# In the attention phase, a projection or a half-chunk stands ahead of the score step in each turn, instead of behind it

## The reference

```python
def fox_prompt(q, k, v, logf):
    c = jnp.cumsum(logf, axis=1).transpose(0, 2, 1)
    ...
    def block(i):
        ...
        s = jnp.einsum('bqhd,bkhd->bhqk', qb, k).astype(jnp.float32) * scale
        s = s + (cb[..., :, None] - c[..., None, :])
        s = jnp.where(qpos[:, None] >= kpos[None, :], s, -jnp.inf)
        p = jax.nn.softmax(s, axis=-1).astype(v.dtype)
        return jnp.einsum('bhqk,bkhd->bqhd', p, v)
...
    m = jax.nn.sigmoid(g_a) * (a @ w_pa) + jax.nn.sigmoid(g_b) * (b @ w_pb)
```

## Time and profile before

| | |
|---|---|
| median of three runs | 1940.32 us |
| profiled execution, its own time | 1940.35 us |
| its span | 1938.6 us |
| TensorE busy | 1886.9 us (97%) |
| VectorE, ScalarE, GpSimd busy | 962.6, 679.1, 521.3 us |
| mean granted TensorE clock | 0.993 |
| chain that ended last: TensorE | 82% |

### The profile page before, as it was taken

The page is one execution under the profiler, slowest core; times in us unless marked ns, Lnnn a source line. Parts: engine busy times, 40 slices in busy tenths (PEclk is TensorE's granted clock), DMA queues, the critical chain, the costliest instruction groups (busy, mean ns, idle before and its releaser), DMA issues.

```text
span 1938.6 us, 30929 instructions
## 1 busy us (share of the span) xinstructions
PE 1886.9 (97%) x11156; PEld 1745.0 (90%) x11156; DVE 962.6 (50%) x2298; ACT 679.1 (35%) x1491; POOL 521.3 (27%) x525
## 2 busy tenths in 40 slices
PE   5999999999999999999999999999999999999998
PEld 4999999999888889998889999999998788999986
DVE  5446565654165335545444566655433643454431
ACT  5344544444233223113224444454432332221120
POOL 3623333433121113211134233333311211231110
PEclk7999999999999999999999999999999999999999
DMA  5231313123224323624324113131322252227151
GB/s 157 58 108 44 100 52 98 52 73 88 68 69 138 98 63 85 201 85 155 113 63 112 53 48 100 45 104 52 100 67 62 77 152 78 77 70 248 38 175 54
DMA packets 217803, 178.39 MB, mean 92 GB/s; under 512 B 50260, under 2 KB 191076, under 8 KB 217652
## 3 DMA queue, kind: packets, MB, share of 16 engines
q1 hardware_dynamic: 217652, 176.41, 31.4%
HBM read 131.65 MB, written 44.71 MB: 91 GB/s over the span
## 4 chain that ended last, share of the span: by engine, by line
PE 82%; DVE 6%; issue 4%; ACT 3%; DMA 2%; POOL 1%; SPq 0%; POOLq 0%; DVEq 0%; ACTq 0%
PE bank L76 22%; PE bank L78 21%; PE bank L77 21%; PE bank L1367 3%; PE bank L1381 2%; PE bank L1327 2%; PE bank L1380 2%; PE bank L1350 2%; PE bank L1352 2%; PE bank L2150 2%; PE bank L2173 1%; DVE sg_sT L1605 1%; DMA at_stage<-in_w_in 1%; DVE at_prob L1247 1%; PE bank L2138 1%
## 5 line engine op out<-in xcount | busy, mean ns | idle before, releaser
L76 PE MATMUL bank<-keep_hhi,at_fhi 128*128 128x384 f32 (+1 forms) x768 | 257.1, 335 | 4.9 <-ACT at_th L1015 4.6
L78 PE MATMUL bank<-keep_hhi,at_flo 128*128 128x384 f32 (+1 forms) x768 | 251.3, 327 | 0.0
L77 PE MATMUL bank<-keep_hlo,at_fhi 128*128 128x384 f32 (+1 forms) x768 | 251.3, 327 | 0.0
L76 PE MATMUL bank<-aw_whi,keep_hhi 128*128 128x384 f32 (+3 forms) x576 | 198.7, 345 | 3.2 <-ACT at_th L1015 1.3
L76 PE MATMUL bank<-keep_hhi,bw_whi 128*128 128x384 f32 (+1 forms) x576 | 195.1, 339 | 2.7 <-DVE br_th L2038 2.7
L77 PE MATMUL bank<-aw_wlo,keep_hhi 128*128 128x384 f32 (+3 forms) x576 | 195.7, 340 | 0.0
L78 PE MATMUL bank<-aw_whi,keep_hlo 128*128 128x384 f32 (+3 forms) x576 | 195.4, 339 | 0.0
L77 PE MATMUL bank<-keep_hlo,bw_whi 128*128 128x384 f32 (+1 forms) x576 | 188.4, 327 | 0.0
L78 PE MATMUL bank<-keep_hhi,bw_wlo 128*128 128x384 f32 (+1 forms) x576 | 188.3, 327 | 0.0
L1061 ACT ACTIVATE at_prob<-at_prob,at_nmx 128x128 f32<-128x128 f32 (+7 forms) x128 | 99.5, 778 | 238.5 <-DVE at_nmx L1254 238.4
L76 PEld LDWEIGHTS bank<-keep_hhi,at_fhi 128*128 128x128 f32 x768 | 144.4, 188 | 8.3 <-ACT at_th L1015 6.9
(11 more groups left out here) (260 smaller groups left out, 4294.0 us busy)
## 6 DMA issues: line engine op xcount, KB each, us to landing
at_stage<-in_w_in SPq DMA_DIRECT2D x160, 128.0 KB, 2.4
mg_gate<-gates SPq DMA_DIRECT2D x32, 544.0 KB, 5.8
gates<-at_th SPq DMA_DIRECT2D x64, 192.0 KB, 2.3
br_stage<-in_w_in SPq DMA_DIRECT2D x40, 256.0 KB, 3.3
at_stage<-in_w_in SPq DMA_DIRECT2D x48, 192.0 KB, 2.7
at_decay<-ncum SPq DMA_DIRECT2D x16, 512.0 KB, 3.8
br_k<-in_cache_k SPq DMA_DIRECT2D x32, 256.0 KB, 3.0
br_v<-in_cache_v SPq DMA_DIRECT2D x32, 256.0 KB, 3.0
```

Of the source, the lines that this page charges most:

```text
L76: nc.tensor.matmul(out, sh, mh, start=start and i == 0, stop=False)
L77: nc.tensor.matmul(out, sh, ml, start=False, stop=False)
L78: last = nc.tensor.matmul(out, sl, mh, start=False, stop=stop and i == n - 1)
```

## The change

In every turn of the loop that has scores or projections due, the order of the two is swapped. Before, a score step came first and a projection (or, between two scores, a half-chunk) behind it. Now the projection comes first, or a half-chunk where no projection is due, and the score step behind it. A half-chunk now also stands ahead of the last score of a turn without projections; the even spread at the end of the turn then asks for one fewer.

```diff
         while scores or projections:
+            if projections:
+                fill.before_z()
+                spent += 2
+                plan.append(projections.pop(0))
+            else:
+                fill.half()
             if scores:
                 s = scores.pop(0)
                 plan.append(s)
                 if s[2] == PT_ - 1 and s[1] + 1 < H:
                     plan.append(("N", s[1] + 1))
-            if projections:
-                fill.before_z()
-                spent += 2
-                plan.append(projections.pop(0))
-            elif scores:
-                fill.half()
```

## The result

The changed kernel takes 1956.33 us (median of 4 runs, 1954.34 to 1957.43), the kernel before 1941.01 us in the same rounds: a ratio of 1.0077, with a 95% interval of 1.0064 to 1.009. It is slower, as forecast, by 15 us in place of 9, and the time lies above the range of 1944.5 to 1955.

The account below looks back on a forecast made before the run. TensorE was taken to set the end. Per layer 6.0 us lost less 1.7 gained is 4.3 net, 8.6 for two layers; on 1940.35 us this gave 1949.0 us, with an 8-in-10 range of 1944.5 to 1955.

Parts of the forecast that it names:

- turns 1 and 2: VectorE and ScalarE chain to Z 1 0: chunk 0.44 us late, S 1 0 adds 0.3; 0.7 us lost per layer.
- The half-chunk moved out of the wait fills other waits: Half-chunk formerly between the values and Z 1 0 in turn 2: moving it was priced at no further loss.
- some 9 us in all: Expected rise of TensorE's waits for ScalarE's tanh, at half-chunks and projections of P 5, P 7 2, P 13 and others.
- I went through all of them and found more than 2 us of room: Other turns with P or Z directly behind the values: no loss expected, except only 0.2 us of room in turn 42.
- Turns 11 to 13: P 4 1 0 no longer hides ScalarE's serial piece of exponential, weight splits, copies and tanh; 2.5 us lost per layer.
- The rival that this piece doesn't bind: Loads of turn 12 may come sooner, so turn 13 costs only 1.0 us; time 1946.0 us, chance 20%.
- the sisters: Turns 25 and 43, same shape as turn 13: P waits for a tanh just ahead, 1.0 us lost each per layer.
- Turns 25, 43, 38, 40 and 23: Waits for tanh lose 1.0 us each in 25 and 43, 0.3 in 38, 0.5 in 40; turn 23 gains 0.7.
- The handoffs: Slower filler matmul behind a score step, 34 times a layer instead of 56; 1.0 us gained per layer.
- the decay row: Load behind Z's key store in turns 7, 19, 31: priced at nothing; late-row rival 1955 us, 15% including other missed waits.
- The faster case: Tanh through by the end of the values, so five places cost nothing; 1937.0 us, or 1933.6; chance 5%.

Follow-up runs that it names:

- filled-wait kernels: Unread matmuls added in the wait ahead of Z 1 0: 14 on the changed kernel (1954.28, again 1952.56 us), 13 with the tanh also before the T steps (1938.03).

## Why the prediction was right in sign and wrong in size

**The step that failed: turns 1 and 2, "0.7 us lost".** The start of Z 1 0 was nearly right: 17.17 us behind T 0 0 0, against 16.61 before, 0.56 later where 0.44 stood in the forecast; without the half clock, layer one would be 0.8 us behind at turn 5, for 0.7. What failed is the sentence "The half-chunk moved out of the wait fills other waits". The forecast put the clock at nothing, without a reason, and its list of waits to come ("some 9 us in all") doesn't have the 3.9 us in which TensorE stands still here. The same work had kept TensorE from standing still for long. The two waits of before, with 2.3 us of score step and half-chunk between them (130.18 to 133.16 less the 0.65 us of idle), became one of 3.9, and the clock behind it fell to half. That is 2.75 and 1.51 us, 4.3 of the 7.0 us by which the turns of the profiled execution (15.6) lie above the forecast (8.6). The median lies 7.3 us above it, of which 0.7 is the kernel before, slower by that in these rounds. The filled-wait kernels show that the clock follows from the standstill: with the order and the start of Z 1 0 kept within 0.3 us and only work put into the wait, Z 1 0 took 4.30 or 4.31 us in six cases of six. The Trainium skill (TensorE: Matmul & The Clock Gate, section Wait — 56ns, not 53.3ns?) gives N / 1.2 GHz between the starts of matmuls at the lower level, for 384 columns an estimate of 0.32 us; the trace agrees, with 0.32.

**Missed: turn 26.** "I went through all of them and found more than 2 us of room" doesn't reach it: the half-chunk that the new order moves into turn 26 waits 0.38 and 0.35 us in the first profile, between nothing and 1.5 in others, and the lag grows by 0.46 and 0.45 us a layer there. I looked at the P steps directly behind the values and not at those that came a turn earlier.

**Turns 11 to 13: right.** Forecast 2.5 us a layer, measured 2.40 and 2.48, and P 5 0 0 starts 12.53 us behind S 2 5 where 12.7 was computed. The rival that this piece doesn't bind is refuted, by the trace and by the kernel with turn 11 in the old order, which takes the piece away and leaves 1.1 us, as at the sisters.

**Turns 25, 43, 38, 40 and 23: right.** By the table, in layer one: 1.15 and 1.06 us in turns 25 and 43, for 1.0 each; 0.27 and 0.63 by turns 38 and 40, for 0.3 and 0.5. In turn 23 0.7 was forecast and 0.76 and 0.74 gained.

**The handoffs: mis-sized.** 1.0 us a layer was forecast. Between turns 13 and 22, where nothing waits, the changed kernel catches up 0.25 us, and between turns 5 and 11 0.08; over the layer it is 0.2 to 0.5, as an estimate from these. The 0.23 us behind L1355 is indeed seen fewer times, but the filler that now stands behind the values takes 0.23 as well where the V ends in 128 columns (18 times in the two layers), and 0.18 behind the wider ones. I priced the handoff that went away and not the one that came for it. By the same estimate this is 1 to 1.6 us of the miss.

**Rivals.** No wait of TensorE for VectorE's release of a Z and none for `at_qn` was seen in the turns, so the decay row was rightly priced at nothing; its 1955 was the nearest number of mine for the wrong reason. The faster case fell: the tanh does not lead the values unless the plan is changed for it.

## What to carry to other kernels

Before a swap that gathers waits, ask how long the engine will stand still in one piece, and what follows would cost at half clock. A small piece of work between two waits can be worth more than its own time (1.8 us moved, 4.4 us gained), and a long wait that can't be avoided can be filled with matmuls that nobody reads; how much of that reaches the end has to be measured. Where an eviction decides, move it ahead of the copies that wait for TensorE before reordering TensorE itself: one line gave 14 us back here in the new order and 5 in the old.

## What the runs showed that I had not expected

- The same standstill of 2.25 us left the clock at full in layer one and halved it in layer two of one execution; and after the same 3.86 us Z 1 0 took 5.80, 6.58 or 7.06 us.
- In the kernels with filled waits the phases behind the turns changed too: in layer two a wait of TensorE for `sg_g`, 0.75 us in the changed kernel run beside them, is gone, and in layer one one of 0.66 to 0.89 us has come. No run shows why.
- Two stores took SyncE 2.40 us to issue in place of 1.01, in another kernel one load 1.54 in place of 0.44; TensorE then waited 1.48 and 1.25 us at P 8 1 0, behind a load, a split and a tanh.
- TensorE's granted clock in the first 38 us was 0.75 to 0.79 in some profiled executions and 1.00 in others of kernels that are alike there, and S 0 0 started anywhere from 104.1 to 107.2 us. The one doesn't explain the other: the starts are 104.1 to 106.0 us at 1.00 and 104.7 to 107.2 below. Neither is part of the change.
